# Conditioning tiles at 1.32 per weight unit in the wide layers, and none left for the last layer

## Chip, core and metric

The kernel runs on one NeuronCore of one Trainium2 chip. The metric is the device time of one execution in microseconds. The kernel before took 3131.53 us (median of 3 runs, 3130.64 to 3136.25).

## What is computed

Two stacks of transformer blocks run over one sequence of 256 positions, width 1024, in float32. The second stack has four layers, and its activations are modulated by vectors that come from a conditioning vector and from a context's conditioning vector, each multiplied with a weight matrix of 1024 by 6144 per layer. The second stack carries 256 more columns of context until its last attention:

```
for i in range(4):
    mod_l = (silu(c) @ mod_w[i] + mod_b[i])        # six vectors of 1024
    mod_c = (silu(c_ctx) @ mod_w[i] + mod_b[i])
    a_l = rmsnorm(x, norm1_g[i]) * (1 + mod_l[1]) + mod_l[0]
    y_l = attention, conformer, short convolution or attention of a_l (and of a_c)
    x = x + mod_l[2] * y_l
    m_l = rmsnorm(x, norm2_g[i]) * (1 + mod_l[4]) + mod_l[3]
    x = x + mod_l[5] * (square(relu(m_l @ mlp_w1[i])) @ mlp_w2[i])
    # the same for ctx with mod_c, for i < 3
```

The first stack (dilated attention, SwiGLU, mLSTM, SwiGLU) has no such vectors. All of `mod_l` and `mod_c` depends on the inputs alone, so it can be computed at any time before its use.

## The kernel before

Activations stay in SBUF with the features in the partitions (`X`, 8 tiles of 128 features by 512 columns, 256 of the sequence and 256 of the context). Every linear layer is cut into units: `linear` (L356) takes a unit of 1024 by 256 weights, 1 MB. SP loads it into one of 3 `raw` buffers (`load`, L1000); ScalarE writes its rounded upper part into `hi` (L1237, L1238) and VectorE (DVE) the rest into `lo` (L1508, L1511), each into one of 2 slots. TensorE then multiplies it with the two halves of the activations: 8 products for each of 2 output tiles, each of three matmuls (L1036 to L1038), 48 in all. The matmuls have 512 columns where the context is carried along, in what is called wide layers below, and 256 columns in the last MLP. Each output tile goes to a bank of PSUM and is taken out by DVE and ScalarE: in the first half of an MLP by L1474, L1876, L1476 and L1878, in the second half and at the end of an attention by the residual (L1554). A split of unit j+1 stands in DVE's order ahead of the takings out of unit j, and waits until unit j-1 is used up.

The conditioning vectors are made by DVE. Their 24,576 rows (4 layers, 6 vectors, 1024 features) are 192 conditioning tiles of 128 rows, 48 to a layer. A tile is one `condition` (L1557): a load of 128 by 1024 weights, 512 KB, by a DMA from the queue of GpSimd (POOL, `mod_load`, L1902) into `MW`, then two multiply-and-sum instructions on DVE (L1562, one for each of the two conditioning vectors), each with a small read of the accumulator. There is one buffer `MW`: the load of tile n+1 is issued when tile n is done. When the tiles of a vector are complete, `mod_close` (L1566) adds the bias and makes the gain `gs` of a norm.

A planner in Python writes all steps in one order before the program is built; each engine then takes its own steps in that order and waits in place. It puts conditioning tiles at two kinds of places:

```
    def beside(self):
        self.credit = min(self.credit + self.pace / 2, 2.0)
        if self.credit >= 1:
            self.credit -= 1
            self.condition()

    def conditions_for(self, layer, i):
        while self.parts < layer * 48 + (i + 1) * 8:
            self.condition()
```

`beside` (L341) is called after each output tile of a unit, so `pace` is the number of conditioning tiles per unit of two output tiles. `conditions_for` (L347) is called ahead of a norm or a residual that needs a vector, and puts all tiles that are still missing in a row at that place. `norm` (L424) calls it for its shift and its gain, `residual` (L441) for its gate. The numbers that set `pace` stand in `plan` (L868). The steps of the second stack, in order, with the number of conditioning tiles in each stage of the kernel before:

| stage | tiles by `beside` | tiles in a row by `conditions_for` |
|---|---|---|
| first stack, attention of layer 0 | 42 | 0 |
| MLP of layer 0 (wide) | 34 | 0 |
| conformer of layer 1 (wide) | 11 | 1 |
| MLP of layer 1 (wide) | 34 | 0 |
| short convolution of layer 2 (wide) | 16 | 0 |
| MLP of layer 2 (wide) | 35 | 0 |
| attention of layer 3 | 3 | 8, ahead of the MLP's norm |
| MLP of layer 3 (256 columns) | 3 | 5, ahead of its first residual |

The MLP (`mlp`, L841) has 32 units, in the order up(0), up(1), down(0), up(2), down(1), up(3), down(2), down(3) of 4 units each; the residual of down(0) is the first to need vector 5.

Of the kernel before, what the change touches and what calls it, by code (L numbers as in the profile page):

```python
# [520 lines left out]
def swiglu(p, layer):  # L521
    s = p.norm(S, ("ffn_norm", layer))
    if layer == 1:
        p.do("context", s)
    x = ("xn", s, 0, S)
    p.do("tables", SILU)
    for j in range(11):
        def evac_g(t, b, u):
            p.do("ffn_gate", layer, j, t, b, u)

        def evac_u(t, b, u):
            p.do("ffn_up", layer, j, t, b, u)

        p.linear("ffn_w_in", layer, 0, KT, j * 256, 256, x, evac_g, outer=j == 0)
        p.linear("ffn_w_in", layer, 0, KT, DFF + j * 256, 256, x, evac_u)
    p.do("tables", LNEXP)
    for c in range(4):
        banks = [p.bank(), p.bank()]
        for k0, kt in ((0, 8), (8, 8), (16, 6)):
            j = p.take("ffn_w_out", layer, k0 * P, kt, c * 256, 256)  # L540
            p.last_unit = j
            for t in range(2):
                for k in range(kt):
                    kk = k0 + k
                    p.do("product", j, t, k, kt, banks[t], ("hf", layer, k0), kk == 0, kk == 21)
                if c < 3:
                    p.beside()
                if k0 + kt == 22:
                    if t == 0:
                        p.flush()  # L550
                    p.residual(c * 2 + t, S, None, *banks[t], True)
# [107 lines left out]
def between(p):  # L659

    p.flush()
    s = p.rstd(S)
    for k in range(KT):
        p.do("block_out", s, k, p.norms)
        p.square(k, 512, 1)
        p.flush()
    p.rs_user = ("block_out", KT - 1)
# [151 lines left out]
def shortconv(p, layer):  # L819
    s = p.norm(512, ("gs", layer, 0), (layer, 0))  # L820
    x = ("xn", s, 0, 512)
    p.do("sc_pads", s)
    for c in range(4):
        def evac_c(t, b, u):
            p.do("sc_c", c, t, b, u)

        def evac_v(t, b, u):
            p.do("sc_v", c, t, b, u)

        def evac_b(t, b, u):  # L830
            p.do("sc_b", c, t, b, u)

        p.linear("sc_win_2", 0, 0, KT, 1024 + c * 256, 256, x, evac_c, outer=c == 0)
        p.linear("sc_win_2", 0, 0, KT, 2048 + c * 256, 256, x, evac_v)
        p.do("sc_conv", c)
        p.linear("sc_win_2", 0, 0, KT, c * 256, 256, x, evac_b)
        p.do("sc_halves", c)
    p.grow(("yh", 0, 0, 512), 512, (layer, 2), "sc_wout_2", 0)


def mlp(p, layer, n):  # L841
    s = p.norm(n, ("gs", layer, 1), (layer, 3))
    x = ("xn", s, 0, n)
    made = [0]

    def up(q):
        for c in range(4):
            def evac(t, b, u):
                p.do("mlp_up", layer, q, 2 * c + t, n, made[0], b, u)
                made[0] += 1  # L850

            p.linear("mlp_w1_2", layer, 0, KT, q * D + c * 256, 256, x, evac, outer=q + c == 0)

    def down(q):
        for c in range(4):
            def evac(t, b, u):
                p.residual(2 * c + t, n, (layer, 5), b, u, q == 3)

            p.linear("mlp_w2_2", layer, q * D, KT, c * 256, 256, ("h2", layer, q, n), evac, quiet=q == 3 and c == 3)

    up(0)
    for q in range(4):
        if q + 1 < 4:
            up(q + 1)
        down(q)


def plan(known):  # L868
    p = Plan(known)
    p.do("begin")  # L870
    for j in range(KT):
        p.square(j, S, 4)
        p.flush()
    p.flush()
    p.ahead_of_all()
    p.do("tables", LNEXP)
    attention(p)
    p.pace = 0.65
    swiglu(p, 0)
    p.pace = 0.0  # L880
    mlstm(p)
    p.pace = 0.65
    swiglu(p, 1)
    between(p)
    p.pace = 0.25
    neighbourhood(p, 0, 0, True)
    p.pace = 1.15
    mlp(p, 0, 512)
    conformer(p, 1)
    mlp(p, 1, 512)  # L890
    shortconv(p, 2)
    mlp(p, 2, 512)
    p.pace = 0.25
    neighbourhood(p, 3, 1, False)
    p.pace = 0.5
    mlp(p, 3, S)
    p.flush()
    p.do("finish", p.rstd(S))
    return p
# [1080 lines left out]
def build(nc, T):  # L1980
    with ExitStack() as ctx:
        m = allocate(nc, ctx)
        p = plan(plan(None).units)
        table = {}
        mute, sig = Mute(), signals(m, table)
# [65 lines left out]
```

## Time and profile before

| | |
|---|---|
| median of 3 runs | 3131.53 us |
| the profiled execution, its own time | 3133.35 us |
| its span in the trace | 3131.5 us |
| TensorE (PE) busy | 2907.9 us, 93% |
| DVE busy | 2003.9 us, 64% |
| ScalarE (ACT) busy | 1188.3 us, 38% |
| POOL busy | 350.8 us, 11% |
| mean granted TensorE clock | 0.968 |

The page gives busy time for each engine and a picture of the span in 40 slices of 78.3 us. Behind it, the trace answers which instruction waited for what (the waits), what each engine did in order of time (the timeline), and how busy each engine was in a given stretch (the windows). PE's busy time overlaps its own pipeline, so a gap on PE shows more than a share does.

### The profile page before, as it was taken

The page shows a single profiled execution, that of the slowest core. Times are in us where ns is not written, and L with a number is a line of the kernel's source. Part 1 is how long each engine was busy: PE and PEld are TensorE (multiplying, and loading weights), DVE is VectorE, ACT ScalarE, POOL GpSimd, SP SyncE. Part 2 cuts the span into 40 slices and gives each one's busy share as a digit, 9 for nine tenths or more (in the row PEclk, how much of TensorE's full clock was granted, in tenths as well). Part 3 has the DMA queues.
Part 4 walks back from the last instruction along what each step waited for, and adds up shares of the span by engine and source line. Part 5 has one row for each costly group of instructions (what it writes and reads, how often), then busy time and mean ns, then how long its engine had stood idle before and what let it go on. Part 6 is the DMA issues. An engine that isn't in the chain of part 4 may idle for free.

```text
span 3131.5 us, 41521 instructions
## 1 busy us (share of the span) xinstructions
PE 2907.9 (93%) x17130; PEld 2486.5 (79%) x17130; DVE 2003.9 (64%) x3252; ACT 1188.3 (38%) x1927; POOL 350.8 (11%) x539
## 2 busy tenths in 40 slices
PE   7999999989999989999998999999999999983778
PEld 7998998889967668888755788878878887773778
DVE  6765777668755556666545766667676666554755
ACT  5444544644444434222314422332242223431434
POOL 0000000000122310000231000010100001431000
PEclk9999999989999999999999999999999999996989
DMA  6443675347745514444453344434434444662443
GB/s 222 148 135 122 213 232 186 120 161 240 237 90 80 81 48 154 149 149 157 136 149 100 124 161 148 155 115 148 157 119 148 153 164 117 113 101 93 163 151 133
DMA packets 362271, 451.80 MB, mean 144 GB/s; under 512 B 12657, under 2 KB 332433, under 8 KB 362081
## 3 DMA queue, kind: packets, MB, share of 16 engines
q1 hardware_dynamic: 326976, 329.89, 32.2%
q0 software_dynamic: 34944, 118.65, 15.3%
q8 instruction: 135, 2.21, 0.3%
q10 hardware_dynamic: 160, 0.59, 0.1%
q14 instruction: 56, 0.45, 0.0%
HBM read 438.67 MB, written 1.05 MB: 140 GB/s over the span
## 4 chain that ended last, share of the span: by engine, by line
PE 83%; DVE 9%; ACT 4%; DMA 2%; issue 1%; POOL 0%; DVEq 0%; ACTq 0%; POOLq 0%
PE ps L1036 24%; PE ps L1038 24%; PE ps L1037 24%; PE ps L1205 2%; DMA MW<-in_mod_w 2%; DVE MX L1562 2%; PE ps L1057 1%; DVE lo L1508 1%; PE ps L1059 1%; PE ps L1058 1%; PE ps L1192 1%; DVE lo L1511 1%; PE ps L1069 1%; PE ps L1180 1%; ACT hi L1237 1%
## 5 line engine op out<-in xcount | busy, mean ns | idle before, releaser
L1036 PE MATMUL ps<-XN,hi 128*128 128x256 f32 (+1 forms) x3008 | 1020.6, 339 | 113.6 <-DVE XN L1534 78.9
L1037 PE MATMUL ps<-XN,hi 128*128 128x256 f32 (+1 forms) x3008 | 1007.2, 335 | 0.0
L1038 PE MATMUL ps<-XN,lo 128*128 128x256 f32 (+1 forms) x3008 | 1006.6, 335 | 0.0
L1036 PEld LDWEIGHTS ps<-XN,hi 128*128 128x128 f32 x3008 | 581.8, 193 | 199.2 <-DVE XN L1534 86.5
L1038 PEld LDWEIGHTS ps<-XN,lo 128*128 128x128 f32 x3008 | 581.8, 193 | 54.3
L1037 PEld LDWEIGHTS ps<-XN,hi 128*128 128x128 f32 x3008 | 582.6, 194 | 52.4
L1508 DVE TENSOR_TENSOR lo<-raw,hi 128x1024 fp32r<-128x1024 f32 (+1 forms) x313 | 384.1, 1227 | 269.8 <-ACT hi L1237 268.2
L1562 DVE CUSTOM_DVE_ANT_0 MX<-MW,C 128x1024 bf16<-128x1024 f32 x384 | 484.0, 1261 | 110.9 <-DMA MW<-in_mod_w 104.1
L1237 ACT ACTIVATE hi<-raw 128x1024 fp32r<-128x1024 f32 (+1 forms) x313 | 326.2, 1042 | 457.2 <-PE ps L1038 456.1
L1036 PE MATMUL ps<-H,hi 128*128 128x512 f32 (+1 forms) x1024 | 372.9, 364 | 28.8 <-DVE lo L1508 28.8
L1511 DVE TENSOR_TENSOR lo<-raw,hi 128x1024 fp32r<-128x1024 f32 (+1 forms) x313 | 380.4, 1215 | 0.0
L1038 PE MATMUL ps<-H,lo 128*128 128x512 f32 (+1 forms) x1024 | 372.6, 364 | 0.0
L1037 PE MATMUL ps<-H,hi 128*128 128x512 f32 (+1 forms) x1024 | 372.5, 364 | 0.0
L1238 ACT ACTIVATE hi<-raw 128x1024 fp32r<-128x1024 f32 (+1 forms) x313 | 324.7, 1037 | 0.0
L1904 POOL DMA_DIRECT2D MW<-in_mod_w x192 | 103.2, 538 | 1576.2 <-DVE mod L1562 1462.6
L1554 DVE SCALAR_TENSOR_TENSOR X<-ps,mod,X 128x256 f32<-128x256 f32 x264 | 116.7, 479 | 195.0 <-PE ps L1038 194.8
L1036 PEld LDWEIGHTS ps<-H,hi 128*128 128x128 f32 x1024 | 194.4, 190 | 59.0 <-issue 29.2
L1037 PEld LDWEIGHTS ps<-H,hi 128*128 128x128 f32 x1024 | 194.4, 190 | 29.9
L1038 PEld LDWEIGHTS ps<-H,lo 128*128 128x128 f32 x1024 | 194.3, 190 | 29.8
L1910 POOL TENSOR_TENSOR SA<-SA,NB 128x256 f32<-128x256 f32 (+1 forms) x75 | 79.6, 1061 | 821.5 <-ACT NB L1245 820.5
L1057 PE MATMUL ps<-hi,XN 128*128 128x256 f32 x512 | 150.5, 294 | 0.1
L1474 ACT ACTIVATE NB<-ps 128x512 f32<-128x512 f32 (+1 forms) x128 | 69.3, 541 | 206.1 <-PE ps L1038 206.1
(225 smaller groups left out, 3401.4 us busy)
## 6 DMA issues: line engine op xcount, KB each, us to landing
raw<-in_mlp_w SPq DMA_DIRECT2D x128, 1024.0 KB, 5.1
MW<-in_mod_w POOLq DMA_DIRECT2D x192, 512.0 KB, 3.8
raw<-in_ffn_w_in SPq DMA_DIRECT2D x44, 1024.0 KB, 5.2
raw<-in_attn_w_in SPq DMA_DIRECT2D x36, 1024.0 KB, 4.8
raw<-in_na_wqkv SPq DMA_DIRECT2D x24, 1024.0 KB, 6.0
raw<-in_ffn_w_out SPq DMA_DIRECT2D x16, 1024.0 KB, 5.6
raw<-in_mlstm_w_in SPq DMA_DIRECT2D x12, 1024.0 KB, 5.1
raw<-in_cv_w SPq DMA_DIRECT2D x12, 1024.0 KB, 7.0
```

The costliest lines, as they stand in the source:

```text
L1036: e.matmul(out, whi, xhi, start=first, stop=False)
L1037: e.matmul(out, whi, xlo, start=False, stop=False)
L1038: i = e.matmul(out, wlo, xhi, start=False, stop=last)
L1057: e.matmul(out, xhi, hi[:, k, :], start=k == 0, stop=False)
L1237: e.activation(hi[:, a:b], raw[:, a:b], ACT.Copy).then_inc(*high.says(("hi", j, 0)))
L1238: e.activation(hi[:, b:c], raw[:, b:c], ACT.Copy).then_inc(*high.says(("hi", j, 1)))
L1508: e.tensor_tensor(lo[:, a:b], raw[:, a:b], hi[:, a:b].bitcast(F32), ALU.subtract).then_inc(*low.says(("lo", j, 0)))
L1511: e.tensor_tensor(lo[:, b:c], raw[:, b:c], hi[:, b:c].bitcast(F32), ALU.subtract).then_inc(*low.says(("lo", j, 1), ("spent", j)))
L1554: e.scalar_tensor_tensor(out=m.X[:, j, a:b], in0=src[:, a:b], scalar=mod_of(m, gate, j, i), in1=m.X[:, j, a:b], op0=ALU.mult, op1=ALU.add) ...
L1562: e.tensor_tensor_reduce(out=m.MX[:, :], in0=m.MW[:, :], in1=m.C[:, s, :], scale=1.0, scalar=0.0, op0=ALU.mult, op1=ALU.add, accum_out=m.m ...
L1904: e.dma_start(m.MW[:, :], T["mod_w_2"][n // 48][n % 48 * P:(n % 48 + 1) * P, :]).then_inc(*sig["mw"].says(("mod_raw", n)))
L1910: e.tensor_tensor(m.SA[:, 0:n], m.SA[:, 0:n], m.SQ[:, i % 2, 0:n], ALU.add).then_inc(*pool.says(("sa", s, i)))
```

## The change

Two numbers in `plan`:

```diff
@@ -884,7 +884,7 @@
     between(p)
     p.pace = 0.25
     neighbourhood(p, 0, 0, True)
-    p.pace = 1.15
+    p.pace = 1.32
     mlp(p, 0, 512)
     conformer(p, 1)
     mlp(p, 1, 512)
@@ -892,7 +892,7 @@
     mlp(p, 2, 512)
     p.pace = 0.25
     neighbourhood(p, 3, 1, False)
-    p.pace = 0.5
+    p.pace = 0.0
     mlp(p, 3, S)
     p.flush()
     p.do("finish", p.rstd(S))
```

The number of conditioning tiles stays 192. By stage they now stand so:

| stage | before | after |
|---|---|---|
| first stack, attention of layer 0 | 42 | 42 |
| MLP of layer 0 | 34 | 39 |
| conformer | 12, one of them in a row | 12 |
| MLP of layer 1 | 34 | 40 |
| short convolution | 16 | 18 |
| MLP of layer 2 | 35 | 40 |
| attention of layer 3 | 11, eight of them in a row | 1 |
| MLP of layer 3 | 8, five of them in a row | 0 |

The order of the instructions on PE, ScalarE and SP is the same in both kernels; only DVE's and POOL's changes. Three places of it follow. In the names, `X` is the residual, `MX` and `mod` are written by a conditioning tile, `lo` is written by a split of weights, `gs` is a norm's gain, `NB<-X,gs,RS` and `XN<-NB,mod,XN` are the norm's scaling and its lower half.

**DVE at the norm of the last MLP.** Before, eight conditioning tiles stand in a row behind the last residual of the attention. Their last one, and what follows:

```order
L1562 ISA MX,mod<-MW,C 128x1024
L1562 ISA mod 128x1
L1562 ISA MX,mod<-MW,C 128x1024
L1562 ISA mod 128x1
L1571 TENSOR_TENSOR mod<-mod,PV 128x16 x2
L1578 SCALAR_TENSOR_TENSOR gs<-mod,PV 128x16
L1520 SCALAR_TENSOR_TENSOR NB<-X,gs,RS 128x256 x3
L1534 SCALAR_TENSOR_TENSOR XN<-NB,mod,XN 128x256
```

In the changed kernel:

```order
L1508 TENSOR_TENSOR lo<-raw,hi 128x1024
L1511 TENSOR_TENSOR lo<-raw,hi 128x1024
L1554 SCALAR_TENSOR_TENSOR X<-ps,mod,X 128x256 x2
L1520 SCALAR_TENSOR_TENSOR NB<-X,gs,RS 128x256 x3
L1534 SCALAR_TENSOR_TENSOR XN<-NB,mod,XN 128x256
```

The norm's first scaling now follows the last residual with nothing between them.

**POOL from the last bias tables of the attention to the end.** Before:

```order
L1942 TENSOR_TENSOR NB<-NB,cst 128x256 x2
L1910 TENSOR_TENSOR SA<-SA,NB 128x256 x2
L1904 DMA MW<-in_mod_w 128x1024
L1910 TENSOR_TENSOR SA<-SA,NB 128x256 x4
L1904 DMA MW<-in_mod_w 128x1024 x15
L1910 TENSOR_TENSOR SA<-SA,NB 128x256 x6
```

In the changed kernel:

```order
L1938 DMA NB<-in_na_rpb 64x4x64 x4
L1942 TENSOR_TENSOR NB<-NB,cst 128x256 x2
L1938 DMA NB<-in_na_rpb 64x4x64 x4
L1942 TENSOR_TENSOR NB<-NB,cst 128x256 x2
L1910 TENSOR_TENSOR SA<-SA,NB 128x256 x12
```

All sixteen loads of conditioning weights from there on are gone.

**DVE in a wide MLP, in the second half of it.** In both kernels a unit has one conditioning tile or two. A unit with one, as it stands in the kernel before in the MLP of layer 2:

```order
L1554 SCALAR_TENSOR_TENSOR X<-ps,mod,X 128x256 x4
L1562 ISA MX,mod<-MW,C 128x1024
L1562 ISA mod 128x1
L1562 ISA MX,mod<-MW,C 128x1024
L1562 ISA mod 128x1
L1508 TENSOR_TENSOR lo<-raw,hi 128x1024
L1511 TENSOR_TENSOR lo<-raw,hi 128x1024
```

A unit with two tiles, from the changed kernel's MLP of layer 2, where it comes round every third unit:

```order
L1554 SCALAR_TENSOR_TENSOR X<-ps,mod,X 128x256 x2
L1562 ISA MX,mod<-MW,C 128x1024
L1562 ISA mod 128x1
L1562 ISA MX,mod<-MW,C 128x1024
L1562 ISA mod 128x1
L1554 SCALAR_TENSOR_TENSOR X<-ps,mod,X 128x256 x2
L1562 ISA MX,mod<-MW,C 128x1024
L1562 ISA mod 128x1
L1562 ISA MX,mod<-MW,C 128x1024
L1562 ISA mod 128x1
L1508 TENSOR_TENSOR lo<-raw,hi 128x1024
L1511 TENSOR_TENSOR lo<-raw,hi 128x1024
```

Ahead of the split there are two conditioning tiles, one of them between the two takings out. Over the five wide stages there are 34 places in the kernel before, and 72 in the changed one, where two successive output tiles both have a conditioning tile.

## Rows read from the trace of the kernel before

**Rows 1.** The page: busy time, and PE's busy tenths in 40 slices.

```profile
PE 2907.9 (93%) x17130; PEld 2486.5 (79%) x17130; DVE 2003.9 (64%) x3252; ACT 1188.3 (38%) x1927; POOL 350.8 (11%) x539
...
PE   7999999989999989999998999999999999983778
```

**Rows 2.** Windows: stretch, length, PE, PEld, DVE, ACT, POOL busy, PEclk, DMA, GB/s.

```profile
2276.00:2634.00 358.00, 353.15 (x1540) 291.02 (x1540) 244.47 (x372) 114.91 (x154) 26.86 (x41) 0.99 0.45 146
...
2853.00:2907.00 54.00, 4.40 (x26) 4.43 (x27) 24.87 (x49) 4.96 (x11) 4.28 (x8) 0.53 0.25 88
...
2960.00:2992.00 32.00, 6.38 (x54) 6.17 (x52) 14.19 (x25) 4.01 (x4) 2.11 (x4) 0.66 0.30 99
```

**Rows 3.** DVE's timeline at the last MLP's norm: start us, us, instruction.

```profile
2850.63 0.48 DVE L1554 SCALAR_TENSOR_TENSOR X<-ps,mod,X 128x256 f32<-128x256 f32 x1 [0.27 <-PE ps L1038]
...
2858.20 1.23 DVE L1562 CUSTOM_DVE_ANT_0 MX<-MW,C 128x1024 bf16<-128x1024 f32 x1 [4.24 <-DMA MW<-in_mod_w]
...
2900.83 1.28 DVE L1520 SCALAR_TENSOR_TENSOR NB<-X,gs,RS 128x256 f32<-128x256 f32 x3
```

**Rows 4.** ACT's timeline at the same norm: the reciprocal root that scaling needs.

```profile
2853.34 0.42 ACT L1252 ACTIVATE RS<-RS 128x256 f32<-128x256 f32 x1
```

**Rows 5.** PE's waits in 2851 to 2907, 2907 to 2960, 2960 to 2996.

```profile
PE ps L1036 <- DVE XN L1534: 49.8, 1, 49.8
...
PE ps L1036 <- DVE lo L1508: 4.0, 3, 1.6
...
PE ps L1036 <- DVE lo L1508: 27.2, 1, 27.2
```

**Rows 6.** Timeline of the last MLP: first weights on PE, splits and last residual on DVE.

```profile
2902.57 0.29 PEld L1036 LDWEIGHTS ps<-XN,hi 128*128 128x128 f32 x1 [50.18 <-DVE XN L1534]
...
2907.66 1.23 DVE L1508 TENSOR_TENSOR lo<-raw,hi 128x1024 fp32r<-128x1024 f32 x1 [0.41 <-ACT hi L1237]
...
2958.74 1.23 DVE L1508 TENSOR_TENSOR lo<-raw,hi 128x1024 fp32r<-128x1024 f32 x1 [0.62 <-ACT hi L1237]
...
3008.40 1.22 DVE L1508 TENSOR_TENSOR lo<-raw,hi 128x1024 fp32r<-128x1024 f32 x1 [0.74 <-ACT hi L1237]
...
3054.48 1.22 DVE L1508 TENSOR_TENSOR lo<-raw,hi 128x1024 fp32r<-128x1024 f32 x1 [0.74 <-ACT hi L1237]
...
3122.38 0.48 DVE L1554 SCALAR_TENSOR_TENSOR X<-ps,mod,X 128x256 f32<-128x256 f32 x1 [2.40 <-PE ps L1038]
```

**Rows 7.** Waits of DVE and PE in the wide MLP of layer 2, 2276 to 2634.

```profile
DVE X L1554 <- PE ps L1038: 50.9, 20, 4.5
...
PE ps L1036 <- DVE XN L1534: 4.0, 1, 4.0
```

**Rows 8.** DVE's timeline in the same MLP: a tile, a taking out, two splits, a pair.

```profile
2432.29 1.22 DVE L1562 CUSTOM_DVE_ANT_0 MX<-MW,C 128x1024 bf16<-128x1024 f32 x1
...
2434.70 0.69 DVE L1876 TENSOR_TENSOR NB<-ps,NB 128x512 f32<-128x512 f32 x1
2436.09 0.69 DVE L1878 TENSOR_TENSOR H<-NB,H 128x512 fp32r<-128x512 f32 x1 [0.70 <-ACT H L1476]
...
2447.82 1.23 DVE L1508 TENSOR_TENSOR lo<-raw,hi 128x1024 fp32r<-128x1024 f32 x1 [0.35 <-ACT hi L1237]
2448.96 1.22 DVE L1511 TENSOR_TENSOR lo<-raw,hi 128x1024 fp32r<-128x1024 f32 x1
...
2458.69 1.23 DVE L1508 TENSOR_TENSOR lo<-raw,hi 128x1024 fp32r<-128x1024 f32 x1 [0.35 <-ACT hi L1237]
...
2468.28 1.23 DVE L1562 CUSTOM_DVE_ANT_0 MX<-MW,C 128x1024 bf16<-128x1024 f32 x1 [0.89 <-DMA MW<-in_mod_w]
```

**Rows 9.** DVE's timeline: the longest wait for a load, in the conformer.

```profile
1564.47 1.23 DVE L1562 CUSTOM_DVE_ANT_0 MX<-MW,C 128x1024 bf16<-128x1024 f32 x1 [15.54 <-DMA MW<-in_mod_w]
```

**Rows 10.** Timelines of DVE and of POOL at the end of layer 2.

```profile
2620.88 2.20 DVE L1562 CUSTOM_DVE_ANT_0 MX<-MW,C 128x1024 bf16<-128x1024 f32 x1
...
2620.45 1.55 POOL L1910 TENSOR_TENSOR SA<-SA,NB 128x512 f32<-128x512 f32 x1 [1.65 <-ACT NB L1245]
```

## Prediction

> **What bounds the kernel now.** I read the page first. PE is busy 93% of the span and DVE 64% [rows 1], so a change that only moves DVE's work pays where PE is not busy. In PE's 40 slices two stand out near the end: the 37th at 3 tenths and the one before it at 8 [rows 1]. The windows put this into stretches: from 2853 to 2907 us PE is busy for 4.4 of 54 us, from 2960 to 2992 for 6.4 of 32, while in a wide MLP (2276 to 2634) it is busy for 353.2 of 358 [rows 2]. PE's waits name the cause: one wait of 49.8 us for the norm's `XN`, and one of 27.2 us for a split of weights `lo` [rows 5]. Both come from DVE, and DVE's timeline shows it waiting in turn: each of the conditioning tiles in a row waits 4.24 us for its load and then works for some 2.4 us [rows 3, 8]. So for these two stretches the bound is a chain of load, two sums, load, two sums through the single buffer `MW`. Everywhere else in the second stack the bound is PE.
>
> A measurement of this kernel tells about 0.2%, 6 us, from no change.
>
> **The row of eight tiles at the norm: minus 47.0 us.** It ends at the norm's first scaling at 2900.83 [rows 3]. Without it, that scaling waits for the reciprocal root, which is ready at 2853.34 + 0.42 = 2853.76 [rows 4]; the last residual before it ends at 2851.11 [rows 3], so nothing else on DVE is later. With some 0.05 us for the signal it starts at 2853.8. All of it lies on the path, since PE has nothing to do before `XN`. What is late next is the root itself, and after it the eight scalings, which stay as they are. `gs` and `mod` of this norm are then made some 200 us earlier, in the MLP of layer 2.
>
> **The row of five and three single tiles in the last MLP: minus 34.3 us.** From the first weights on PE at 2902.57 to the last residual at 3122.38 there are 219.8 us [rows 6]. Where no tile stands in it, this MLP goes at PE's pace: eight units from 3008.40 to 3054.48, or 5.76 us a unit [rows 6], and 32 units are 184.3. I add 1.2 us: the first unit is paced by DVE's `XN` and runs partly at a lower granted clock, as it does now. That makes 185.5. As a check, the two waits for `lo` in it sum to 27.2 + 4.0 = 31.2 [rows 5]; the rest of the 34.3 is the slow start behind the long gap, where the granted clock is 0.66 over the window, between its two levels of 1.2 and 2.4 GHz [rows 2]. Could DVE hold PE even without tiles? From 2907.66 to 2958.74 there are eight splits' intervals, three of them with a tile: 51.1 us [rows 6], less three tiles of 2.4 is 43.9, or 5.5 a unit, under PE's 5.76. So DVE keeps up, with little to spare.
>
> **The attention of layer 3: minus 1 us.** It loses two of its three single tiles. At most all of them were on the path, 2 x 2.4 = 4.8 us, at least none; I take 1, near none, since this stretch is held by other chains and its remaining tile stays.
>
> **The wide layers: 18 tiles more, costed at 0.** From 2432.29 to the next instruction at 2434.70 a tile takes 2.41 us of DVE [rows 8], so 18 make 43.4 us. They lie beside PE's work: in the MLP of layer 2, DVE waits 50.9 us for PE at the residuals alone, and PE's one wait is 4.0 us for the norm [rows 7]. But a mean is not enough, so I take the densest stretch, the first half of an MLP, unit by unit. A unit takes 10.87 us on PE (2447.82 to 2458.69) [rows 8]. On DVE it costs a split of 2 x 1.14 = 2.3 us (two starts 1.14 apart) and two takings out of 2.0 us (2434.70 to 2436.09 + 0.6) [rows 8]. Three units then have 3 x 6.3 = 18.9, and four tiles now 9.6. Only where both tiles of a unit follow each other with nothing but a taking out between them, the second waits for its load: 4.24 less 2.0 is 2.2 us [rows 3, 8]. Where a split lies between, it covers the load. The sum is 30.7 us against PE's 32.6: 94% full. Before, with 3.45 tiles and a pair in every second such stretch, it was some 28.3, or 87%. It still fits, and a split that starts late has most of a unit until PE needs it. So 0, and the cover is 1.9 us in three units. If it is gone, each in-unit pair's 2.2 us and each added tile's 2.4 come out on PE; the upper bound is below. Nothing below 0 either: PE has no wait there that a tile could take away.
>
> Two places I looked at singly. In the conformer a load stood behind POOL's spreading of `U` and DVE waited 15.54 us [rows 9] without holding PE; the changed kernel has a tile at the same place. It also puts one behind the last `U`, ahead of three small sums that PE needs: I see room of 1 to 2 us, cost 0 to 3. POOL's own queue gets 18 loads more here and 18 fewer later, and POOL is 11% busy [rows 1].
>
> At the end of layer 2 a sum that should take 1.22 us took 2.20: it began at 2620.88, while POOL's addition ran from 2620.45 to 2622.00 [rows 10]. The Trainium skill (SBUF — State Buffer, section SBUF: two separate sides) states that VectorE and GpSimd share a pair of ports, that an instruction with two SBUF inputs on the one and one on the other exclude each other, and that the loser blocks fully. By that rule, the trace agrees.
>
> **The sum.** 47.0 + 34.3 + 1 = 82.3 us off the profiled execution's span of 3131.5 gives 3049.2. That execution took 3133.35 us, 1.85 more than its span, and lies 1.8 above the median of 3131.53. The two cancel: against the median I say **3049.5 us**, 2.6% faster.
>
> **The rivals.**
>
> *Half hidden.* The pairs' waits reach PE in the wide layers. There are 38 more pairs, half of them within a unit: 19 x 2.2 = 42 us, so about 3091. For it: 94% is tight, and real DVE times scatter. Against it: no wait of DVE for a load in a wide layer reached PE before, not even the one of 15.54 us. 10%.
>
> *Held at the ends of stages.* POOL's additions of squares and the tiles' sums hold each other. Each collision costs 1.0 us (2.20 less 1.22) [rows 10]; the four wide stages that end in a residual have some two more tiles each in their last eight units, so 8 us if all of it delays the norm: 3057.5. This is what the rule on the ports, taken by itself, would make of it. Against: the last unit carries no tile (`quiet`), and the norm waits for the last residual. 5%.
>
> *Another wait steps in* in the last layer: loads, or DVE's 5.5 us chain turning out at 6 us a unit. 32 x 0.24 = 8 us: 3057. Against: units without tiles run at 5.76 now. 5%.
>
> *It does not do what it says*: some tiles are still missing at the last norm and stand there in a row again. The order of the instructions shows none there, so this takes a misreading of it: 3131, 1%.
>
> *Slower.* The wide layers turn over: DVE becomes the bound in them. Then all 18 tiles come out, 43 us, the 19 pairs within units with 2.2 and the 19 across with 1.0 (0.89 in the rows) [rows 8], 42 + 19. That is 104 us lost against 82 gained: 3153. It decides from the point at which 79% of DVE's added time reaches PE. Since tiles in layers bound by PE have all been hidden so far [rows 7], 2%.
>
> **The numbers.** The forecast has 77%. Its own spread: the attention's 0 to 4.8, the first unit's start by 1.5, the conformer's 0 to 3, some microseconds of unseen late splits: 3044 to 3057. To reach to the neighbours at 3057 I take the range to 3066, and below to 3043; that leaves out the half hidden case, no change and slower, 13%, and a little of the forecast. Faster by over 0.2%: 77 + 10 + 5 + 5 = 97%, of which I keep 96; within 0.2% 1; slower 3, with the unknown.
>
> **What would show it.** PE's two waits of 49.8 and 27.2 us [rows 5] are gone, and no tile stands behind the attention. From the last MLP's first weights on PE to its last residual there are 185 to 186 us, with splits 5.76 apart from the second unit on. Each wide MLP keeps its length (2276 to 2634 is one) within 1 us, and PE waits in it only for `XN`; DVE's waits for loads about double, to 15 to 20 us per MLP. Wrong would be a wait of PE for `lo` in a wide MLP, or a wide MLP that is longer by over 3 us.

## The result and the profile after

| | before | changed |
|---|---|---|
| median of four runs each | 3133.8 us (3130.64 to 3136.25) | 3062.12 us (3060.76 to 3063.12) |
| profiled execution, and its span in the trace | 3133.35, 3131.5 us | 3061.46, 3059.6 us |
| PE busy | 2907.9 us, 93% | 2913.1 us, 95% |
| DVE busy | 2003.9 us | 2002.2 us |

The ratio is 0.9772, with a 95% interval of 0.9755 to 0.9788: 2.3% faster, 71.7 us. The prediction counted from the 3131.53 us of the first three runs of the kernel before. The forecast was 3049.5 with a range of 3043 to 3066. The time lies inside the range and 12.6 us above the forecast; the direction and most of the size came true, and the 12.6 us are what the experiments had to explain.

The page of the changed kernel, busy time and PE's slices, to be laid beside [rows 1]:

```profile
PE 2913.1 (95%) x17130; PEld 2489.8 (81%) x17130; DVE 2002.2 (65%) x3252; ACT 1188.7 (39%) x1927; POOL 357.2 (12%) x539
...
PE   7998999979999989999999899999999999998898
```

The hole at 3 tenths is gone. DVE does the same work; it does it elsewhere. DVE's timeline at the last MLP's norm, where [rows 3] had the row of eight:

```profile
2860.84 0.48 DVE L1554 SCALAR_TENSOR_TENSOR X<-ps,mod,X 128x256 f32<-128x256 f32 x1 [1.01 <-PE ps L1038]
2863.52 1.28 DVE L1520 SCALAR_TENSOR_TENSOR NB<-X,gs,RS 128x256 f32<-128x256 f32 x3 [2.19 <-ACT RS L1252]
```

The scaling comes 2.7 us after the last residual starts, and waits for the reciprocal root, as foreseen. PE's waits from 2860 to the end of the last MLP, where [rows 5] had 49.8 and 27.2:

```profile
PE ps L1036 <- DVE XN L1534: 2.8, 1, 2.8
PE ps L1069 <- ACT NB L1245: 0.6, 1, 0.6
PE ps L1066 <- POOL SA L1910: 0.3, 1, 0.3
```

No wait for `lo` is left in it. From the first weights on PE to the last residual:

```profile
2865.27 0.19 PEld L1036 LDWEIGHTS ps<-XN,hi 128*128 128x128 f32 x1 [3.14 <-DVE XN L1534]
...
3050.49 0.48 DVE L1554 SCALAR_TENSOR_TENSOR X<-ps,mod,X 128x256 f32<-128x256 f32 x1 [2.40 <-PE ps L1038]
```

These are 185.2 us, where 185.5 were forecast and 219.8 were needed before [rows 6]. The wide MLP of layer 2, windows and PE's waits (against [rows 2, 7]):

```profile
2282.00:2640.00 358.00, 353.18 (x1540) 290.93 (x1540) 256.04 (x393) 114.91 (x154) 29.49 (x46) 0.99 0.47 153
```

```profile
PE ps L1036 <- DVE XN L1534: 4.0, 1, 4.0
PE ps L1069 <- ACT NB L1245: 0.8, 1, 0.8
```

DVE is busy 256.0 us in it instead of 244.5, and PE waits for nothing more than before.

To see where the rest went, I measured each stage in every trace, from the first scaling of its norm (the first L1520 on DVE) to that of the next one, and the last MLP to the final scaling (L1884). All in us:

| kernel | up to MLP 0 | MLP 0 | conformer | MLP 1 | short conv. | MLP 2 | attention 3, with the row | last MLP |
|---|---|---|---|---|---|---|---|---|
| before | 1142.2 | 357.1 | 220.7 | 356.7 | 183.4 | 357.9 | 267.0 | 224.2 |
| changed | 1146.6 | 357.7 | 221.4 | 356.7 | 183.4 | 357.9 | 223.9 | 189.7 |
| forecast, as a difference | 0 | 0 | 0 | 0 | 0 | 0 | -48.0 | -34.3 |
| measured difference | +4.4 | +0.6 | +0.7 | 0.0 | 0.0 | 0.0 | -43.1 | -34.5 |

The measured differences sum to -71.9 us, which is the difference of the two spans. Against the forecast's -82.3, 4.9 us are missing in the attention of layer 3 with its row, 4.4 us in front of MLP 0, where the two kernels have the same instructions in the same order, and 1.3 in MLP 0 and the conformer; the last MLP gave 0.2 more.

### The profile page after: what moved, and what is told of

Same layout as the page of the kernel before. It is cut to its first block, busy times and chain, and to the rows that moved or that the text cites. A ratio compares the mean times of both kernels' runs of the same rounds, so it can differ in the third digit from the quotient of the medians.

```text
span 3059.6 us, 41515 instructions
## 1 busy us (share of the span) xinstructions
PE 2913.1 (95%) x17130; PEld 2489.8 (81%) x17130; DVE 2002.2 (65%) x3252; ACT 1188.7 (39%) x1927; POOL 357.2 (12%) x539
## 4 chain that ended last, share of the span: by engine, by line
PE 85%; DVE 7%; ACT 4%; DMA 1%; issue 1%; POOL 1%; DVEq 0%; ACTq 0%; POOLq 0%
PE ps L1036 25%; PE ps L1037 25%; PE ps L1038 25%; PE ps L1057 2%; PE ps L1059 1%; PE ps L1058 1%; PE ps L1205 1%; DVE lo L1508 1%; DVE lo L1511 1%; PE ps L1192 1%; PE ps L1069 1%; PE ps L1180 1%; DVE NB L1520 1%; DMA NB<-in_na_rpb 1%; PE ps L1101 1%
## 5 line engine op out<-in xcount | busy, mean ns | idle before, releaser
L1036 PEld LDWEIGHTS ps<-H,hi 128*128 128x128 f32 x1024 | 193.3, 189 | 29.8
L1058 PE MATMUL ps<-lo,XN 128*128 128x256 f32 x512 | 145.6, 284 | 0.0
```

Source lines behind the costliest of these rows:

```text
L1036: e.matmul(out, whi, xhi, start=first, stop=False)
L1058: e.matmul(out, xhi, lo[:, k, :], start=False, stop=False)
```

## Experiments

Three questions were put. Does each of the two removed rows bring what was charged to it? Where do the missing microseconds lie? And how far does the cover in the wide layers reach, and what ends it? All diffs are against the changed kernel where nothing else is said. Each time stands beside runs of the kernel before in the same comparison (medians 3134.41, 3135.86 and 3135.44).

### The row at the norm alone

The dense pace, but the last eight tiles are kept back for the last MLP, at the old pace there (diff against the kernel before):

```diff
-        self.last_unit = None
+        self.last_unit, self.limit = None, 184
-        if self.credit >= 1:
+        if self.credit >= 1 and self.parts < self.limit:
-    p.pace = 1.15
+    p.pace = 1.32
-    p.pace = 0.5
+    p.pace, p.limit, p.credit = 0.5, 192, 0.0
```

> The changed kernel, but no more than 184 tiles are made ahead of the last MLP; the last eight stand in it as in the kernel before (three single, five in a row at its first residual), and none stands at its norm. Theory (each row of tiles is a serial chain on the path, the wide layers are free): the norm's 47 us stay gained, the 34 us of the last MLP are lost again, so about 3062 + 34 = 3096 us, with the last MLP at 219 to 220 us from its first weights on PE to its last residual. Rival (the row at the norm hid something else that would now appear, or the gain came from the freed load queue): over 3105 us, or under 3085.

Measured: 3088.27 us, ratio 0.9851 (0.9834 to 0.9868), 8 us under the expected 3096 and 26 above the changed kernel. The spans of the two profiled executions differ by 29.6 us, of which 32.6 are the last MLP; this kernel has no tile in attention 3 and seven fewer in MLP 2, and saves 1.4 and 1.3 there. Attention 3 takes 222.5 us, so the row's part is gone; the last MLP takes 222.3, 1.9 less than before and 32.6 more than in the changed kernel. PE's waits in the last MLP of this kernel:

```profile
PE ps L1036 <- DVE lo L1508: 28.6, 3, 26.8
PE ps L1036 <- DVE XN L1534: 2.8, 1, 2.8
```

The two parts are separate. The wait for `lo` stays at 28.6 us without the row ahead of it (31.2 with it [rows 5]), so it belongs to the tiles in the last MLP.

### A longer row

The kernel before, with the last pace at 0 and the tiles of one more vector called for at the norm, so that sixteen stand there in a row (diff against the kernel before):

```diff
-            self.conditions_for(shift[0], shift[1] + 1)
+            self.conditions_for(shift[0], shift[1] + 1 + (shift == (3, 3)))
-    p.pace = 0.5
+    p.pace = 0.0
```

> The kernel before, with all of the last sixteen tiles in one row at the norm of the last MLP and none in that MLP (its three single ones and its row of five are moved up). Theory (a tile in a row costs a fixed 6.6 us: 4.1 for its load, 2.4 for its sums; a single tile hidden beside PE or nearly so): the row grows by 8 x 6.6 = 53 us to about 102 us, the last MLP loses its tiles and takes 190 us from the norm's scaling to the last scaling, so 3134 - 34 + 53 = 3153 us. Rival (the load's wait in a row is an effect of other traffic and shrinks, as SP's weight loads have stopped by then): under 5.5 us a tile, 3140 or less.

Measured: 3151.9 us, ratio 1.005 (1.0032 to 1.0067). Attention 3 with the row takes 318.1 us against 267.0, 51.1 us for eight tiles more, 6.4 a tile; the last MLP takes 191.6. The starts on DVE in this row are 6.4 to 6.7 us apart (the first two 7.0), of which some 4 are the wait:

```profile
2857.91 1.23 DVE L1562 CUSTOM_DVE_ANT_0 MX<-MW,C 128x1024 bf16<-128x1024 f32 x1 [4.02 <-DMA MW<-in_mod_w]
...
2864.44 1.22 DVE L1562 CUSTOM_DVE_ANT_0 MX<-MW,C 128x1024 bf16<-128x1024 f32 x1 [4.04 <-DMA MW<-in_mod_w]
...
2871.09 1.22 DVE L1562 CUSTOM_DVE_ANT_0 MX<-MW,C 128x1024 bf16<-128x1024 f32 x1 [4.14 <-DMA MW<-in_mod_w]
```

A tile in a row costs its whole chain. This kernel has no tile in its last MLP and is still 0.5% slower than the one before: what counts is whether a tile has cover, not in which stage it stands.

### No tile in the last attention

```diff
-    p.pace = 1.32
+    p.pace = 1.34
```

> The changed kernel with 1.34 in place of 1.32: one more tile in the wide layers and none in the attention of layer 3. Theory (the one tile left in the attention, which stands ahead of its first scores, costs about 4 us by holding the bias tables on POOL and the softmax behind it): this attention takes 219 to 220 us from norm to norm, in place of 223.9, and the total is about 3058 us. Rival (the 12 us short of the forecast come from the wide layers and more tiles there cost more): attention unchanged at 224, total 3062 or above.

Measured: 3058.85 us, ratio 0.9756 (0.9742 to 0.9771). Attention 3 takes 219.5 us where the changed kernel takes 223.9. The two timelines of DVE show what stood there. In the changed kernel:

```profile
2680.14 1.75 DVE L1562 CUSTOM_DVE_ANT_0 MX<-MW,C 128x1024 bf16<-128x1024 f32 x1
...
2681.94 1.64 DVE L1562 CUSTOM_DVE_ANT_0 MX<-MW,C 128x1024 bf16<-128x1024 f32 x1
...
2683.79 0.69 DVE L1765 CUSTOM_DVE_ANT_0 PB<-ps,NB 128x512 f32<-128x512 f32 x1
```

In the kernel without it:

```profile
2680.88 0.68 DVE L1765 CUSTOM_DVE_ANT_0 PB<-ps,NB 128x512 f32<-128x512 f32 x1
```

The stages begin at 2639.6 and 2639.8, so the first scores of the first head are taken out (L1765) 3.1 us later, and with them the softmax, PE's turns and the next heads. The two sums take 1.75 and 1.64 us instead of 1.23. This delay is no scatter: L1765 starts 44.2 us into the stage in both traces of the changed kernel, and 40.8 to 41.1 us in all twelve others. In the kernel before the first of the three tiles stood 12 us further on, behind a copy of the turned scores, and L1765 was not delayed. Its three single tiles cost nothing that shows: up to its last residual this attention takes 216.8 us with them, and 216.8 in the kernel without any.

### The tile one place later

```diff
-    p.pace = 0.25
+    p.pace, p.credit = 0.25, 0.0
     neighbourhood(p, 3, 1, False)
```

> The changed kernel with the tile in the attention of layer 3 standing 24 DVE rows later, behind the takings out and softmaxes of its first group; nothing else differs. Theory (the place of that tile ahead of the first scores is what costs): the attention takes 220 to 221 us in place of 223.9, total about 3059 us. Rival (a tile costs the same wherever it stands in the attention, or the 4 us come from something else): 224 us and 3062.

The carried-over credit is set to nothing, and the one tile then stands 60.3 us into the stage where it stood at 40.5.

Measured: 3059.18 us, ratio 0.9761 (0.9744 to 0.9779); attention 3 takes 221.3 us. Laying PE's timelines beside the one without a tile, the changed kernel is 2.5 us late by the turns (L1180, PE's transposes of the scores) at 69 us into the stage, and this one 1.5 us. So the tile costs 1.5 to 2.5 us directly, at either place. That is not all of the 4.4. In time this kernel, the one without a tile and the changed one have intervals that overlap.

### The changed kernel and the one before, once more

> The changed kernel once more, for a second profile. Theory (the first stack, whose instructions are in the same order in all these kernels, varies by some us from one execution to the next, so that 4 of the 12 us short of the forecast are scatter): attention of layer 3 again 223 to 225 us, first stack and attention of layer 0 anywhere from 1157 to 1165 us. Rival (the changed kernel's first stack is slower by something fixed, as its program is another one): again 1162 to 1163 us.

> The kernel before once more, for a second profile. Theory (scatter): the time up to the norm of the MLP of layer 0 anywhere from 1157 to 1165 us, attention of layer 3 again 219 to 221 us up to its last residual. Rival (fixed difference): again 1158.

Measured: 3061.92 us for the changed kernel (four executions: 3068.38, 3053.03, 3058.07, 3065.77), ratio 0.976 (0.9736 to 0.9785); 3132.39 us for the one before. Attention 3 takes 223.9 us again, and the last MLP 190.7. In the second trace of the changed kernel the norm of MLP 0 starts at 1168.5 us, above the 1157 to 1165 of the theory and the 1163 of the rival alike; in the kernel before it starts at 1158.4, which both allow. The attention of layer 3 of the kernel before takes 216.6 us up to its last residual, as in its first trace (216.8) and not the 219 to 221 expected.

From its first norm to that of MLP 0 the changed kernel thus takes 1146.6 and 1152.6 us, the kernel before 1142.2 and 1142.6. The other kernels with the same instructions up to there take 1139.7 to 1148.5, so a fixed difference of 4.4 us is not shown, and the scatter is larger than it. Where it comes from shows best in the first stage of all, the dilated attention, in which every kernel here has the same instructions in the same order. It takes 302.2 us in one trace of the changed kernel and 305.5 in the other; over all 14 traces of this study it lies between 299.0 and 305.6. Windows of that stage, before and then the changed kernel once more (the last columns are the granted clock, the DMA share and GB/s):

```profile
16.00:320.00 304.00, 282.65 (x2203) 276.24 (x2204) 203.71 (x350) 140.35 (x238) 4.41 (x6) 0.98 0.45 149
```

```profile
16.00:320.00 304.00, 285.38 (x2187) 278.23 (x2188) 199.40 (x338) 137.03 (x229) 4.40 (x6) 0.95 0.44 146
```

The granted clock is 0.98 in one and 0.95 in the other, and PE is busy longer by as much as the stage is: 280.1 of 299.8 us in the first, 285.8 of 305.5 in the other. A lower clock shows in the last attention of the changed kernel too, where PE resumes after a wait of 2.04 us:

```profile
2752.09 0.28 PE L1059 MATMUL ps<-hi,XN 128*128 128x256 f32 x1
2754.41 1.97 PE L1180 MATMUL ps<-cst,PB 128*128 128x128 f32 x8 [2.04 <-DVE PB L1780]
2756.03 0.56 PE L1057 MATMUL ps<-hi,XN 128*128 128x256 f32 x1
2756.39 0.41 PE L1058 MATMUL ps<-lo,XN 128*128 128x256 f32 x1
```

At the same place the kernel without the tile, whose wait was 1.98 us, goes on at full speed:

```profile
2752.05 1.09 PE L1180 MATMUL ps<-cst,PB 128*128 128x128 f32 x8 [1.98 <-DVE PB L1780]
2752.90 0.37 PE L1057 MATMUL ps<-hi,XN 128*128 128x256 f32 x1
2753.10 0.28 PE L1058 MATMUL ps<-lo,XN 128*128 128x256 f32 x1
```

A matmul takes 0.41 us in the one and 0.28 in the other, and the lag behind it grows by some 1.3 us here. From 2755 to 2760 the granted clock is 0.73 in the changed kernel, a mix of its two levels of 1.2 and 2.4 GHz. So the attention's lag over the kernel without a tile is 2.5 us of tile and some 2 us more: 1.5 up to the end of this stretch and the rest in small steps behind it. In both traces of the changed kernel all of it stands at the same places, within 0.3 us; whether the later start brings this stretch about stays open. Such stretches come without any tile too: the run at 1.6 below has none in this stage, the same instruction order there as the 219.5 us kernel, and takes 224.1. Six more traces without a tile there lie between 219.1 and 222.5.

### Denser: 2.0 and 1.6

```diff
-    p.pace = 1.32
+    p.pace = 2.0
```

> The changed kernel with 2.0 in place of 1.32: two tiles in every unit of the MLPs of layers 0 and 1 and of the conformer, until all are made early in layer 2. Theory (a unit costs DVE 2.3 for the split, 4.0 for two takings out in the first half of an MLP or 1.6 in the second, 4.8 for two tiles and 2.2 to 3.4 for the load's wait, so 13.3 or 12.3 us against PE's 10.9): both MLPs become bound by DVE and take 395 to 425 us in place of 356.7, and the total is 3130 to 3190 us. Rival (DVE has room for any number of tiles there): both stay at 357 and the total is about 3058 us.

Measured: 3221.67 us, ratio 1.0269 (1.0252 to 1.0287). MLP 0 and MLP 1 take 430.3 and 430.7 us, 72.6 and 74.0 more.

```diff
-    p.pace = 1.32
+    p.pace = 1.6
```

> The changed kernel with 1.6 in place of 1.32. Theory (in the first half of an MLP three units now cost DVE 18.9 for splits and takings out, 4.8 x 2.4 = 11.6 for tiles and 1.5 to 1.8 waits of 2.2 for a load within a unit, so 34 to 34.5 us against PE's 32.6): DVE becomes the bound in the first half only, 16 units lose 0.5 to 0.7 us each, the MLPs of layers 0 and 1 take 360 to 372 us in place of 357.5, total 3065 to 3085. Rival (the edge lies higher, DVE still fits): 357.5 and 3059.

Measured: 3096.56 us, ratio 0.9874 (0.9858 to 0.989). MLP 0 takes 371.1, MLP 1 368.2, the short convolution 200.8 with 23 tiles. At 1.6 the MLPs came out as expected, but the short convolution is 17.4 us longer and the total lies above the 3085 allowed; at 2.0 the MLPs too are beyond the expected 425 us. Both totals fell short: my account of DVE's time left something out. DVE's waits in MLP 0 show what. At 2.0:

```profile
DVE MX L1562 <- DMA MW<-in_mod_w: 94.2, 45, 3.4
DVE H L1878 <- ACT H L1476: 22.3, 32, 0.7
```

With 302.8 us busy this makes 419 of 430 us: DVE is full, and a fifth of it is waiting for loads. At 1.6 the waits for loads are 53.4 us, in the changed kernel 15.4, in the one before 7.3. DVE's timeline at 1.6 in MLP 0 shows the period:

```profile
1255.50 1.23 DVE L1562 CUSTOM_DVE_ANT_0 MX<-MW,C 128x1024 bf16<-128x1024 f32 x1 [2.05 <-DMA MW<-in_mod_w]
...
1262.09 1.22 DVE L1562 CUSTOM_DVE_ANT_0 MX<-MW,C 128x1024 bf16<-128x1024 f32 x1 [1.03 <-DMA MW<-in_mod_w]
...
1268.64 1.23 DVE L1562 CUSTOM_DVE_ANT_0 MX<-MW,C 128x1024 bf16<-128x1024 f32 x1 [3.26 <-DMA MW<-in_mod_w]
...
1275.32 1.22 DVE L1562 CUSTOM_DVE_ANT_0 MX<-MW,C 128x1024 bf16<-128x1024 f32 x1 [0.33 <-DMA MW<-in_mod_w]
...
1281.91 1.23 DVE L1562 CUSTOM_DVE_ANT_0 MX<-MW,C 128x1024 bf16<-128x1024 f32 x1 [1.03 <-DMA MW<-in_mod_w]
```

The tiles start 6.6 us apart, whatever stands between them: a split does not hide the load, it only shortens the wait, because one buffer forces load and sums to alternate. PE's unit of 10.87 us [rows 8] has room for 10.87 / 6.6 = 1.65 such chains. At 2.0 the unit must grow to 2 x 6.6 = 13.2 us; 30 of them and two without tiles are 418, near the 430 measured. At 1.6 the chain is 97% full, at 1.32 it is 80%. The mean is not the edge itself, though: at 1.6 it still fits, and 14 us were lost. Tiles come there in runs of four successive output tiles, one called for every 5.4 us, so that each run falls behind.

What PE loses at 1.6 in MLP 0 is in part waits for `lo` (4.9 us) and one for POOL's sum (3.2), in part 5.9 us more of busy time than in the changed kernel (358.9 against 353.0), at a granted clock of 0.98 instead of 0.99. At 2.0 the waits for `lo` are 46.3 us.

### The same without the loads

If this is right, the same sums at the same places cost nothing once the loads are away. Only the first load is made; all tiles sum over it (beside the edit of the pace to 1.6, and likewise to 2.0):

```diff
-            self.do("mod_load", n + 1)
+            pass
-        w.wait_ge(("mod_raw", n), "silu_c")
+        w.wait_ge(("mod_raw", 0), "silu_c")
```

> The run with 1.6 tiles per unit, with only the first load of conditioning weights; every later tile sums over what stands in MW, so the conditioning vectors are not the reference's. DVE's instructions and their order are those of the 1.6 run. There DVE waited 53.4 us for loads in the MLP of layer 0, was busy 275 us of 371, and the MLP took 371.1 us. Theory (a full chain on DVE, of which the loads are the part that does not fit): the wide MLPs fall back to 356 to 359 us, the short convolution from 200.8 to about 183 to 186, and the time is 3052 to 3064 us. Rival (DVE's own work, or the splits that stand behind two tiles, hold TensorE): the MLPs stay at 365 or more and the time at 3080 to 3097.

> The same with 2.0 tiles per unit: two tiles in every unit, only the first load made, vectors not the reference's. In the run with loads DVE was busy 303 us, waited 94 us for loads and 22 us for ScalarE in an MLP of 430 us: full. Without the 94 us the chain is 336 us long, under 357. Theory of the full chain: the wide MLPs take 357 to 363 us and the time is 3050 to 3075 us. Rival (two tiles ahead of each split make the splits late, loads or not): MLPs of 385 us or more and a time above 3120.

Measured: 3055.94 us at 1.6 (ratio 0.9749, 0.9736 to 0.9762), 40.6 us less than with loads, and 3058.02 at 2.0 (0.9755, 0.9741 to 0.9768), 163.7 less. MLP 0 takes 356.6 and 358.1 us. The windows of MLP 0 at 2.0, with loads and then without (columns as in [rows 2]):

```profile
1157.00:1587.00 430.00, 374.78 (x1540) 298.56 (x1540) 302.76 (x476) 111.75 (x155) 39.65 (x66) 0.96 0.48 152
```

```profile
1157.00:1515.00 358.00, 353.31 (x1540) 291.02 (x1540) 303.02 (x476) 114.84 (x155) 8.97 (x6) 0.99 0.29 94
```

DVE is busy for the same 303 us in both. DVE's own work is no limit at 60 tiles in an MLP; the load chain is. Leaving the loads out also takes 58 GB/s off the DMA engines, so these runs alone can't tell the wait for a load from the traffic that it makes. The traces can. A load of `MW` takes 3.7 us from issue to landing (the median) in this MLP at 2.0, at 152 GB/s, and 3.7 in the row of sixteen, at 80 GB/s. DVE's busy time is the same with and without the loads, and it waits 0.4 us in all for the `hi` of the weights in either run. With loads PE waits for `lo`, made by DVE, and DVE for `MW`: it is the wait.

### 1.45

```diff
-    p.pace = 1.32
+    p.pace = 1.45
```

> 1.45 in place of 1.32 in the wide layers: 43, 44 and 30 tiles in the three wide MLPs, none in the last attention. Theory of the full chain: from 39 tiles in the MLP of layer 0 (busy 254, loads 15.4 us) to 48 (275, 53.4) a tile costs 6.5 us of DVE's chain, and about 61 us of the chain were waits for TensorE and ScalarE at 39 tiles; four more take 26 of them: the MLPs stay within 3 us of 357, the time is 3055 to 3068. Rival (1.32 stands just under an edge): each MLP 363 us or more, the time above 3070.

Measured: 3062.7 us, ratio 0.9772 (0.9759 to 0.9785), the same as at 1.32. MLP 0 and MLP 1 take 356.6 and 357.0 with 43 and 44 tiles, although DVE's waits for loads have doubled to 29.8 us. Here the chain is 88% full. So in the MLPs 1.32 doesn't stand at an edge; that lies between 1.45 and 1.6. The short convolution is nearer: 188.2 us with 20 tiles, 183.4 with 18.

### None in either attention

Four numbers, so that neither neighbourhood attention has a tile:

```diff
-    p.pace = 0.65
+    p.pace = 0.68
-    p.pace = 0.65
+    p.pace = 0.68
-    p.pace = 0.25
+    p.pace = 0.0
-    p.pace = 1.32
+    p.pace = 1.34
-    p.pace = 0.25
+    p.pace = 0.0
```

> No conditioning tile in the attention of layer 0 nor in that of layer 3: 0.68 per unit in place of 0.65 in the two SwiGLUs, 0 in place of 0.25 ahead of both neighbourhood attentions, 1.34 in the wide layers. If a tile that stands ahead of a softmax's first step costs 1 to 3 us there as well, the attention of layer 0 (284 to 289 us so far) takes 281 to 285, that of layer 3 about 219.5, and the time is 3053 to 3058. Rival (in the attention of layer 0 the tiles are covered): no difference from the run with none in the last attention, 3058 to 3061.

Measured: 3067.14 us, ratio 0.9784 (0.9771 to 0.9797). A miss: no gain, 8 us above the kernel at 1.34; from the changed kernel the intervals don't separate it. The profiled execution is the fastest of the five, and its span lies only 1.4 us above that of the kernel at 1.34, so the trace shows one stage that is longer, and not the whole of the 8 us. The attention of layer 0 did not shorten (285.2 us); its tiles are covered. And the shifted tiles met the short convolution, which takes 190.5 us with the same 19 tiles with which the kernel at 1.34 takes 183.4. PE's timeline at the place, and windows around it:

```profile
2235.91 0.39 PE L1038 MATMUL ps<-YH,lo 128*128 128x512 f32 x1
2240.98 0.74 PE L1036 MATMUL ps<-YH,hi 128*128 128x512 f32 x1 [4.68 <-DVE YH L1870]
2241.52 0.63 PE L1037 MATMUL ps<-YH,hi 128*128 128x512 f32 x1
```

```profile
2236.00:2241.00 5.00, 0.32 (x3) 0.02 (x1) 3.15 (x6) 0.87 (x1) 0.38 (x1) 1.00 0.20 76
2241.00:2246.00 5.00, 5.00 (x15) 3.97 (x16) 3.67 (x5) 0.63 (x1) 0.14 (x1) 0.66 0.46 141
2246.00:2251.00 5.00, 5.00 (x24) 4.14 (x23) 1.28 (x3) 0.37 (x1) 0.00 (x0) 1.00 0.49 174
```

PE waits 4.7 us for `YH`, which DVE makes from the convolution's sums. DVE in turn stands before it at the second of two successive tiles, and waits for its load:

```profile
2231.22 1.21 DVE L1562 CUSTOM_DVE_ANT_0 MX<-MW,C 128x1024 bf16<-128x1024 f32 x1
...
2233.63 0.69 DVE L1864 TENSOR_TENSOR CO<-ps,CO 128x512 f32<-128x512 f32 x1
2237.82 1.23 DVE L1562 CUSTOM_DVE_ANT_0 MX<-MW,C 128x1024 bf16<-128x1024 f32 x1 [3.51 <-DMA MW<-in_mod_w]
...
2240.24 1.29 DVE L1870 TENSOR_TENSOR YH<-CO,YH 128x512 fp32r<-128x512 f32 x2
```

The two tiles start 6.6 us apart again. At 1.34 a single tile stands ahead of this `YH`. PE then finds a granted clock of 0.66 over the next 5 us: 15 matmuls instead of 24. At 1.34 the same wait was 0.7 us. Laid beside that kernel, PE is 1.5 us late ahead of this wait (a stretch at lower clock behind the norm) and 7.1 us late once its matmuls run at 0.39 us again: 4.0 us of wait and 1.6 of clock.

No version that makes all the vectors beats the changed kernel by more than the intervals: the two nearest, none in the last attention and the tile one place later, have intervals that overlap its own.

## Why the prediction was right, and by what it was off

**The row of eight at the norm, -47.0 us: right.** The scaling now waits for the root alone, and starts 2.7 us after the last residual where it started 50.2 us after it: -47.5. A tile of a row, 4.24 and 2.4 us in the prediction, came to 6.4 in the longer row.

**The last MLP, -34.3 us: right.** 185.2 us from first weights to last residual against 185.5, and -34.5 by stages. Most of it is the tiles, as said: with the tiles kept and the row gone, the wait for `lo` stays and the stage is 1.9 us shorter. The 3.1 us put down to a slow start are not shown, since this stage lies between 189.6 and 191.7 us in the kernels that have no tile in it. The detail on the splits was off: the first six intervals are 5.47 us, and only from the eighth on does PE's 5.76 show.

**The attention of layer 3, -1 us: the step that failed.** Up to its last residual it takes 221.2 us against 216.8: +4.4, 5.4 off. The forecast's 1 us wasn't there to gain: with its three single tiles the attention before takes no longer than one without any, 216.8 us. For the loss, I argued that "its remaining tile stays". A tile stays in the count but not in its place: the credit left over from the wide layers puts it directly ahead of the first head's scores, where it delays the whole chain of heads by 2.5 us. I had read the order of the instructions at three other places and not at this one. The remaining 2 us are mostly a stretch at the lower clock after a wait of PE, which kernels have or don't have at places where their instructions are the same; that the tile's delay brings it about is not excluded.

**Everything ahead of MLP 0, 0 us: +4.4 in the profiled pair.** No cause in the change was found: the same instructions stand there, and this stretch varies from 1139.7 to 1152.6 us from trace to trace, its first stage with the granted clock. The forecast had nothing for that. Of the 10.4 us by which the span lies over the forecast's 3049.2, 4.4 lie here, 5.4 in the last attention (2.5 of them the tile, some 2 what follows it, 1 the gain that wasn't there) and 1.3 in MLP 0 and the conformer, less 0.7 that the row and the last MLP gave beyond the forecast. The other 2.2 of the 12.6 us come from the step from span to median: the profiled execution of the kernel before lay 1.8 us above the median taken, that of the changed kernel 0.7 below its own, less the 0.3 by which the sum of 3049.2 had been rounded up to 3049.5. That all this adds up to no more than 12.6 us is in part luck, for single executions of the changed kernel lie between 3053 and 3068 us. Why one execution gets the lower clock at a place and another not stays open.

**The wide layers, 0 us: right, with a wrong reason for how near the edge was.** MLP 1, the short convolution and MLP 2 kept their lengths to a tenth, MLP 0 and the conformer came 0.6 and 0.7 longer, inside their scatter (the conformer takes 219.6 and 219.7 in two runs with the same tiles). DVE's waits for loads came to 15.4, 19.7 and 17.0 us in the three wide MLPs, as said (15 to 20). But "94% full" was not a measure of anything: DVE's own work fits even at 2.0 tiles a unit, which by that count would be over 100%. The limit is the load chain, at 80% with 1.32, 88% with 1.45 and 97% with 1.6, where it no longer fits everywhere. And "where a split lies between, it covers the load" was wrong as an argument for density, since the chain of 6.6 us passes through every split. It did no harm at 1.32.

**The rivals.** Half hidden (3091) is near what 1.6 gives (3096.6), and slower (3153) lies on the way to 2.0; at 1.32 neither holds. Held at the ends of the stages: PE waited for POOL's sum at the end of MLP 0 and of the short convolution at 1.6, 3.2 and 2.9 us, and at the end of each of the first three wide stages at 2.0, 5.1 to 5.2 us, but in no wide stage of the changed kernel. The time of 3057 of the third rival was near, but its place was wrong: the last layer's splits keep up.

The second edit of the change, 0.5 to 0.0, has no effect of its own: all 192 tiles are made by then.

## What to carry to other kernels

The side work that runs here beside PE is limited by its serial chain per item, load and two sums through one buffer at 6.6 us, and not by its engine's busy time. Divide the main engine's unit by such a chain for a bound on how many items fit, and stay some way under it where the items come unevenly: the bound was 1.65, and 1.6 already lost 14 us in an MLP. Moved work must be followed to the exact instruction ahead of which it now stands, above all at the start of a latency-bound stage: one tile ahead of the first softmax cost 2.5 us, eighteen more tiles beside matrix products 1.3 us at most. And when two kernels differ by a few microseconds, measure first the stages that are identical in both, since they show what the difference is worth.

## What the runs showed of the hardware

A wait of TensorE can cost more than its length. After the wait of 4.7 us for `YH` the granted clock was 0.66 for the next 5 us, matmuls of 128x512 took 0.63 us instead of 0.39, and a wait that was 4.0 us longer cost 5.6. After waits near 2 us it was the one or the other: with 2.04 us the following matmuls took 0.41, with 1.98 they took 0.28. The same instructions made a first stage of 299.0 us in one execution, at a granted clock of 0.98, and 305.5 in another, at 0.95. In the last attention, on the other hand, two executions of the changed kernel agreed within 0.3 us at every matmul.

The two sums of the tile in the changed kernel's last attention took 1.75 and 1.64 us, against 1.23 otherwise. POOL's timeline has an addition of bias tables beside them:

```profile
2679.88 2.61 POOL L1942 TENSOR_TENSOR NB<-NB,cst 128x256 f32<-128x256 f32 x2 [8.52 <-DMA NB<-in_na_rpb]
```

The Trainium skill (SBUF — State Buffer, section SBUF: two separate sides) states that a VectorE instruction with two inputs in SBUF and a GpSimd instruction that reads SBUF exclude each other. The rows agree, with 0.5 and 0.4 us lost on the two sums here, where it was 1.0 in [rows 10].
